# The eight blocks of each recurrence turn in 512-column matmuls, with VectorE adding the halves

## The chip, the cores and the metric

The kernel runs on one core of a Trainium2 chip. The core has TensorE (PE in the profile; its weight loads are PEld), VectorE (DVE), ScalarE (ACT), GpSimd (POOL) and SyncE (SP), which issues most transfers. The metric is the device time of one launch in microseconds. Three runs of the kernel before took 3868.46 to 3870.62 us, median 3868.93.

## What is computed

Two blocks of a network on 256 tokens of width 2048, in float32. The part that matters here is the first block, which has two layers; each projects the normed input to the inputs of a gated delta rule with 16 heads of width 128, and runs it in chunks of 64 tokens:

```python
h = rmsnorm(x, norm_w) * (1.0 + scale[:, None, :]) + shift[:, None, :]
u = h @ w_in
qkv_a, beta_a, a_a, z_a, q_b, k_b, v_b, z_b, g_a, g_b = split_cols(u, SPLIT_SIZES)
qkv_a = jax.nn.silu(causal_conv(qkv_a, conv_w)).astype(jnp.float32)
...
q_a = l2norm(q_a) * (GDN_HEAD_DIM ** -0.5)
k_a = l2norm(k_a)
...
o_a = gated_delta_rule(q_a, k_a, v_a, g, beta)
o_a = rmsnorm(o_a, gdn_norm_w).reshape(b, s, GDN_WIDTH).astype(x.dtype) * jax.nn.silu(z_a)
```

Sliding-window attention, output products and a second block follow; the change doesn't touch them.

## The kernel before

**Products in parts.** A float32 product of weights W and activations x is made of fp32r parts: W is split into `Wh` and `Wl` = W - `Wh`, and x into a high and a low part. Three products count: `Wh`·x_high, `Wh`·x_low and `Wl`·x_high. The activations lie in `H` as [slab, part, token], so that the high and low parts of a slab of 128 rows are 512 adjacent columns. There are two forms. `pe_half` (L262) makes three 256-column matmuls per slab (L283, L284, L285) and sums all three in the left 256 columns of a PSUM bank. `pe_wide` (L288) makes one 512-column matmul (L300: `Wh` against both parts; the low part's product falls in the right half of the bank) and one of 256 columns (L301: `Wl` against the high part, into the left half). The bank's halves then have to be added, which `dve_tile` (L345, L349) does with a VectorE sum of 512 elements to 256.

**The stream.** Weights come in blocks of 128 output columns by 2048 rows, 8 KB per partition, and each block is worked in two halves of 8 slabs. SyncE fetches blocks into the four places of `raw`. ScalarE casts a half to `Wh` (`act_cast`, L356), VectorE subtracts (`dve_low`, L362), and TensorE multiplies. `Wh` and `Wl` are rings of four halves. While TensorE works on half n, ScalarE and VectorE prepare half n + 4 into the place that TensorE left last. A finished block stands in bank `G[b % 2]`; whoever takes it out increments `tile_taken`, and TensorE begins the block after next only then.

**A turn of the recurrence.** `pe_gdn`, `act_gdn`, `dve_gdn` and `pool_gdn` run side by side. For each of the two layers there are nine turns: the first (`chain` false) only makes projections, the next seven (a loop, `fresh` and `chain` true) make the projections of head pair i while the delta rule of pair i - 1 runs between them, and the ninth (`fresh` false) makes eight gate blocks beside the last pair's delta rule. A turn has eight blocks (q, k and v for two heads each go to `cin`, z to `zin`), so 16 halves, n = 0 to 15. The chain's steps are written into the halves by hand: `before(n)`, `between(n)` after four slabs, `after(n)` after six. In halves 2 to 6 the inverse of a 64 x 64 triangular block is doubled in size: TensorE L1077 makes a product, VectorE masks it (L1330), TensorE L1106 makes a second, VectorE puts it in place with a predicated copy (L1361) and sums it (L1365) for the next half's L1077. Half 8 gives the state (`S`, L1383), half 9 and 10 `vn` (L1339) and the output (L1056), half 12 the squares' sums of the next pair's q and k (`sq_lo`, L1434, then L1135), half 14 the normed q and k (`qkn`, L1419), with which the next turn begins (the gram product, L1064). The conv steps of the next pair (L1312, L1315) fill VectorE's remaining places.

**Order.** Each engine works its instructions in written order. ScalarE takes out each of the eight blocks: in odd halves, after its cast, it copies the left 256 columns to `cin` or `zin` (L1251), or in the ninth turn takes tanh of them (L1256). In a chained turn VectorE's `dve_low` runs one half late: iteration n holds that of half n - 1, and the sixteenth stands behind the loop. At the end of a fresh turn ScalarE waits until the last block is taken (L1258).

## Time and profile before

| | |
|---|---|
| median of three runs | 3868.93 us |
| profiled execution | 3868.1 us |
| its span | 3866.3 us |
| TensorE busy | 3729.4 us, 96% |
| VectorE busy | 2856.1 us, 74% |
| ScalarE busy | 1905.5 us, 49% |
| a chained turn of the recurrence | 61.8 us |

Times in the rows below are in microseconds from the start of the span. A row of the timeline gives start, duration, engine, line of the kernel, operation, what is written and read, the shape, and how many equal ones it merges; in brackets stands the idle time of the engine before it and what ended it. TensorE's matmuls overlap in the trace (each lasts longer than the distance to the next), so its pace is read from start to start. A row of the busy table gives the stretch, its length, and busy time (with the number of instructions) of PE, PEld, DVE, ACT and POOL, then the granted clock, the share of the transfer engines and GB/s.

### The profile page before, as it was taken

To read this page: it belongs to the slowest core of one execution; us is meant where nothing else is said; L and a number is where in the kernel's file an instruction comes from. 1 tells how busy PE (TensorE), PEld (TensorE's weight loads), DVE (VectorE), ACT (ScalarE), POOL (GpSimd) and SP (SyncE) were. 2 spreads that over 40 slices of the span, in tenths; PEclk is the share of its full clock that TensorE was granted. 3 is DMA by queue.
4 is the path that set the end of the run, shared out by engine and by line. 5 is a ranking of instruction groups with operands and counts; after the bars stand their busy time and mean duration, and the time that the engine had idled before them with its cause. 6 is when DMAs were issued, how large, how long until landed. Compare 5 with 4: busy or idle time off the path is not lost.

```text
span 3866.3 us, 70292 instructions
## 1 busy us (share of the span) xinstructions
PE 3729.4 (96%) x27254; PEld 3491.6 (90%) x27254; DVE 2856.1 (74%) x3924; ACT 1905.5 (49%) x2898; POOL 175.7 (5%) x184
## 2 busy tenths in 40 slices
PE   1999999999999999999999999999999999999998
PEld 1999999899988999999989998999987899989988
DVE  8788887867779778888686776665576666666676
ACT  1556565335544355555534554454565433434365
POOL 0111111000000012121000000000000000000000
PEclk8999999999999999999999999999999999999999
DMA  9544444864468844434486444544534555555543
GB/s 396 177 149 146 142 146 139 303 234 164 157 234 318 299 148 142 150 137 152 146 317 214 158 157 175 186 169 175 183 124 149 185 185 185 185 185 185 185 146 127
DMA packets 138700, 720.49 MB, mean 186 GB/s; under 512 B 37697, under 2 KB 38145, under 8 KB 62337
## 3 DMA queue, kind: packets, MB, share of 16 engines
q1 hardware_dynamic: 111456, 631.31, 45.8%
q10 hardware_dynamic: 27040, 86.32, 6.6%
q8 instruction: 146, 2.39, 0.2%
q14 instruction: 58, 0.47, 0.0%
HBM read 711.22 MB, written 2.16 MB: 185 GB/s over the span
## 4 chain that ended last, share of the span: by engine, by line
PE 75%; DVE 13%; issue 5%; ACT 4%; DMA 2%; DVEq 1%; ACTq 0%; SPq 0%
PE bank L300 17%; PE bank L283 11%; PE bank L284 11%; PE bank L285 11%; PE bank L301 9%; DVE Wl L362 3%; PE bank L2416 2%; PE bank L2415 2%; PE bank L2414 2%; ACT Wh L356 2%; DMA raw<-in_ada 1%; DVE gm_more L1315 1%; PE bank L1077 1%; PE bank L326 1%; PE bank L322 1%
## 5 line engine op out<-in xcount | busy, mean ns | idle before, releaser
L356 ACT CAST Wh<-raw 128x1024 fp32r<-128x1024 f32 x1124 | 1170.9, 1047 | 1603.2 <-PE bank L285 905.6
L362 DVE TENSOR_TENSOR Wl<-raw,Wh 128x1024 fp32r<-128x1024 f32 x1124 | 1380.0, 1231 | 701.4 <-ACT Wh L356 698.9
L283 PE MATMUL bank<-H,Wh 128*128 128x256 f32 x4928 | 1444.9, 293 | 2.0 <-DVE Wl L362 1.2
L284 PE MATMUL bank<-H,Wh 128*128 128x256 f32 x4928 | 1393.8, 283 | 0.0
L285 PE MATMUL bank<-H,Wl 128*128 128x256 f32 x4928 | 1393.1, 283 | 0.0
L283 PEld LDWEIGHTS bank<-H,Wh 128*128 128x128 f32 x4928 | 942.4, 191 | 24.6 <-issue 13.7
L284 PEld LDWEIGHTS bank<-H,Wh 128*128 128x128 f32 x4928 | 943.0, 191 | 8.0 <-issue 4.8
L285 PEld LDWEIGHTS bank<-H,Wl 128*128 128x128 f32 x4928 | 942.1, 191 | 0.0
L300 PE MATMUL bank<-H,Wh 128*128 128x512 f32 x2112 | 746.9, 398 | 4.6 <-DVE WS L349 4.5
L301 PE MATMUL bank<-H,Wl 128*128 128x256 f32 x2112 | 592.6, 281 | 0.0
L300 PEld LDWEIGHTS bank<-H,Wh 128*128 128x128 f32 x2112 | 396.7, 188 | 103.2 <-DVE Wl L362 5.7
L301 PEld LDWEIGHTS bank<-H,Wl 128*128 128x128 f32 x2112 | 398.9, 189 | 0.0
L300 PE MATMUL bank<-O,Wh 128*128 128x512 f32 x896 | 317.2, 397 | 6.6 <-DVE both L349 6.3
L301 PE MATMUL bank<-O,Wl 128*128 128x256 f32 x896 | 251.0, 280 | 0.0
L300 PEld LDWEIGHTS bank<-O,Wh 128*128 128x128 f32 x896 | 168.0, 188 | 50.1 <-DVE Wl L362 6.8
L2415 PE MATMUL bank<-O,Wh 128*128 128x256 f32 x704 | 199.2, 283 | 0.0
L2416 PE MATMUL bank<-O,Wl 128*128 128x256 f32 x704 | 199.2, 283 | 0.0
L2414 PE MATMUL bank<-O,Wh 128*128 128x256 f32 x704 | 199.2, 283 | 0.0
L301 PEld LDWEIGHTS bank<-O,Wl 128*128 128x128 f32 x896 | 169.2, 189 | 0.0
L2414 PEld LDWEIGHTS bank<-O,Wh 128*128 128x128 f32 x704 | 135.1, 192 | 0.5
L2416 PEld LDWEIGHTS bank<-O,Wl 128*128 128x128 f32 x704 | 135.1, 192 | 0.0
L2415 PEld LDWEIGHTS bank<-O,Wh 128*128 128x128 f32 x704 | 135.1, 192 | 0.0
(413 smaller groups left out, 4169.8 us busy)
## 6 DMA issues: line engine op xcount, KB each, us to landing
raw<-in_stream SPq DMA_DIRECT2D x560, 1024.0 KB, 4.8
WS<-in_ada ACTq DMA_DIRECT2D x94, 512.0 KB, 6.3
raw<-in_ada SPq DMA_DIRECT2D x32, 1024.0 KB, 7.5
gm_more<-in_ada ACTq DMA_DIRECT2D x20, 512.0 KB, 7.4
WS<-rows_d ACTq DMA_DIRECT2D x16, 512.0 KB, 5.2
KR<-in_ada ACTq DMA_DIRECT2D x14, 512.0 KB, 7.2
raw<-in_stream SPq DMA_DIRECT2D x8, 512.0 KB, 6.9
gm_more<-WS ACTq DMA_DIRECT2D x32, 128.0 KB, 4.8
```

The lines of the kernel that those rows point to most:

```text
L283: pe.matmul(out[:, 0:T], wh, xh[:, kt, :], start=first, stop=False)
L284: pe.matmul(out[:, 0:T], wh, xl[:, kt, :], start=False, stop=False)
L285: mm = pe.matmul(out[:, 0:T], wl, xh[:, kt, :], start=False, stop=last)
L300: pe.matmul(out[:, :], wh, x[:, kt, :, :], start=kt == 0, stop=False)
L301: mm = pe.matmul(out[:, 0:T], wl, x[:, kt, 0, :], start=False, stop=kt == KT - 1)
L322: pe.matmul(out[:, :], wh, x[:, kt, :, :], start=first, stop=False)
L326: mm = pe.matmul(out[:, 0:T], wl, x[:, kt, 0, :], start=False, stop=last)
L356: act.copy(Wh[:, n % 4, :], raw[:, (sbk + 2) % 4, k * (D // 2):(k + 1) * (D // 2)]).then_inc(hi_ready, 1)
L362: dve.tensor_tensor(Wl[:, n % 4, :], raw[:, (sbk + 2) % 4, k * (D // 2):(k + 1) * (D // 2)], Wh[:, n % 4, :].bitcast(F32), ALU.subtract).t ...
L2414: pe.matmul(o, wh, ah, start=x == 0, stop=False)
L2415: pe.matmul(o, wh, al, start=False, stop=False)
L2416: m = pe.matmul(o, wl, ah, start=False, stop=x == 3)
```

## The change

The eight blocks of a fresh turn use `pe_wide` in place of `pe_half`; `pe_wide` learns to call `between` and `after` at the same slabs. ScalarE no longer copies these blocks out. VectorE does, with `dve_tile`, right behind the `dve_low` of the block's second half: in a chained turn that is in even iterations (block b in iteration 2b + 2) and, for block 7, behind the loop. The writes wait for the reads of the turn before (the conv's last step, and `zs` for block 6). The ninth turn keeps `pe_half` and ScalarE's tanh, which now waits on `tile_taken` for its first block, since VectorE took the block before.

```diff
--- before.py
+++ after.py
@@ -285,7 +285,7 @@
                 mm = pe.matmul(out[:, 0:T], wl, xh[:, kt, :], start=False, stop=last)
             mm.then_inc(half_used, 1)
 
-        def pe_wide(pe, q, sbk, k, fill, bank, x, tiles=None):
+        def pe_wide(pe, q, sbk, k, fill, bank, x, tiles=None, between=None, after=None):
 
             out = G[bank]
             pe.wait_ge(lo_ready, q * 8 + (2 * sbk + k + 1))
@@ -293,6 +293,10 @@
                 pe.wait_ge(tile_taken, fill + 1)
             s = (2 * sbk + k) % 4
             for j in range(KT // 2):
+                if j == KT // 4 and between:
+                    between()
+                if j == KT // 4 + 2 and after:
+                    after()
                 kt = k * (KT // 2) + j
                 if tiles and kt % 4 == 0:
                     tiles(kt // 4)
@@ -1154,7 +1158,10 @@
                 if chain:
                     before(n)
                 b, k = n // 2, n % 2
-                pe_half(pe, q + b // 4, b % 4, k, l * TILES + 4 + i * 8 + b, b % 2, Hh, Hl, between=lambda: between(n), after=lambda: after(n))
+                if fresh:
+                    pe_wide(pe, q + b // 4, b % 4, k, l * TILES + 4 + i * 8 + b, b % 2, H, between=lambda: between(n), after=lambda: after(n))
+                else:
+                    pe_half(pe, q + b // 4, b % 4, k, l * TILES + 4 + i * 8 + b, b % 2, Hh, Hl, between=lambda: between(n), after=lambda: after(n))
 
         def act_gdn(act, l, i, fresh, chain):
             S, F, q = st_gdn, st_fr, l * Q_LAYER + Q_PRE + 2 * i
@@ -1243,15 +1250,10 @@
                     front(n)
                 b, k = n // 2, n % 2
                 act_cast(act, q + b // 4, b % 4, k)
-                if k and fresh:
-                    if chain and b == 6:
-                        S.wait(act, "dve", "zs", r)
-                    act_tile(act, q + b // 4, b % 4)
-                    dst = cin[:, b, 3:3 + T] if b < 6 else zin[:, b - 6, :]
-                    act.copy(dst, G[b % 2][:, 0:T]).then_inc(tile_taken, 1)
-                elif k:
+                if k and not fresh:
                     if b == 0:
                         F.wait(act, "dve", "qkn", r)
+                        act.wait_ge(tile_taken, l * TILES + 4 + i * 8 + 2)
                     act_tile(act, q + b // 4, b % 4)
                     act.activation(gates8[:, b, :], G[b % 2][:, 0:T], ACT.Tanh, scale=0.5).then_inc(tile_taken, 1)
             if fresh:
@@ -1421,6 +1423,15 @@
                     F.wait(dve, "act", "tanh_v", f)
                     F.done(dve.scalar_tensor_tensor(cs[:, 4:6, :], tv, 1.0, cs[:, 4:6, :], ALU.add, ALU.mult), "dve", "silu_v")
 
+            def tile(b):
+
+                if chain and b < 6:
+                    F.wait(dve, "dve", f"conv{b}_3", r)
+                if chain and b == 6:
+                    S.wait(dve, "dve", "zs", r)
+                dst = cin[:, b, 3:3 + T] if b < 6 else zin[:, b - 6, :]
+                dve_tile(dve, q + b // 4, b % 4, l * TILES + 4 + i * 8 + b, b % 2, dst)
+
             for n in range(16):
                 if chain:
                     before(n)
@@ -1432,15 +1443,19 @@
                             continue
                         F.wait(dve, "act", f"sq{h}", f)
                         F.done(dve.tensor_tensor(sq_lo[h], tm2[:, 2 * h:2 * h + 2, :], sq_hi[h].bitcast(F32), ALU.subtract), "dve", f"sq_lo{h}")
-                if n or not chain:
-                    late = 1 if chain else 0
+                late = 1 if chain else 0
+                if n >= late:
                     dve_low(dve, q + (n - late) // 8, (n - late) // 2 % 4, (n - late) % 2)
+                if fresh and n >= late and (n - late) % 2:
+                    tile((n - late) // 2)
                 if chain:
                     after(n)
                 if fresh:
                     front(n)
             if chain:
                 dve_low(dve, q + 1, 3, 1)
+                if fresh:
+                    tile(7)
```

In the program of the kernel before, VectorE's rows around the subtraction in half 2 of the looped turn (Wl from raw and Wh), then the predicated copy of the doubling step:

```order
L361 REGISTER_ALU
L362 TENSOR_TENSOR Wl<-raw,Wh 128x1024 [waits hi_ready]
L121 REGISTER_ALU
L1360 MEMSET SEC_X 1x1 [waits gdn_pe_done]
L1361 COPY_PREDICATED WS<-C,bank 128x128x2
L121 REGISTER_ALU
L1365 TENSOR_REDUCE WS<-WS 128x32x2 [waits gdn_dve_done]
```

The same place in the kernel after:

```order
L365 REGISTER_ALU
L366 TENSOR_TENSOR Wl<-raw,Wh 128x1024 [waits hi_ready]
L351 REGISTER_ALU [waits gdn_front_dve_done]
L352 ISA [waits half_used]
L353 TENSOR_REDUCE Y<-bank 128x256 [waits tile_taken]
L121 REGISTER_ALU
L1362 MEMSET SEC_X 1x1 [waits gdn_pe_done]
L1363 COPY_PREDICATED WS<-C,bank 128x128x2
L121 REGISTER_ALU
L1367 TENSOR_REDUCE WS<-WS 128x32x2 [waits gdn_dve_done]
```

The sum of the bank's halves (L353) now stands between the subtraction and the predicated copy.

VectorE at half 14 of the looped turn, before, with the subtraction for half 13, `qkn` (Y from gm_more) and the next subtraction:

```order
L361 REGISTER_ALU
L362 TENSOR_TENSOR Wl<-raw,Wh 128x1024 [waits hi_ready]
L121 REGISTER_ALU
L121 REGISTER_ALU [waits gdn_front_act_done]
L1419 TENSOR_TENSOR Y<-gm_more 128x1024 [waits gdn_pe_done]
L361 REGISTER_ALU
L362 TENSOR_TENSOR Wl<-raw,Wh 128x1024 [waits hi_ready]
```

And after:

```order
L365 REGISTER_ALU
L366 TENSOR_TENSOR Wl<-raw,Wh 128x1024 [waits hi_ready]
L121 REGISTER_ALU
L353 TENSOR_REDUCE Y<-bank 128x256 [waits tile_taken,half_used,gdn_dve_done]
L121 REGISTER_ALU
L121 REGISTER_ALU [waits gdn_front_act_done]
L1421 TENSOR_TENSOR Y<-gm_more 128x1024 [waits gdn_pe_done]
L365 REGISTER_ALU
L366 TENSOR_TENSOR Wl<-raw,Wh 128x1024 [waits hi_ready]
```

The sum of block 6 stands ahead of `qkn`, L1421 in the new numbering.

ScalarE at the end of the looped turn, before, with the casts of halves 14 and 15, the copy of block 7, the loop's branch and the first steps of a turn:

```order
L355 REGISTER_ALU [waits raw1_landed]
L356 CAST Wh<-raw 128x1024 [waits half_used]
L1251 COPY Y<-bank 128x256 [waits half_used]
L1258 ISA
L2714 REGISTER_ALU [waits tile_taken]
L2714 COMPARE_AND_BRANCH
L1171 ACTIVATE WS<-Y 128x512
L1172 ACTIVATE WS<-WS 128x512
```

And after:

```order
L359 REGISTER_ALU [waits raw1_landed]
L360 CAST Wh<-raw 128x1024 [waits half_used]
L1260 ISA
L2729 REGISTER_ALU [waits tile_taken]
L2729 COMPARE_AND_BRANCH
L1178 ACTIVATE WS<-Y 128x512
L1179 ACTIVATE WS<-WS 128x512
```

The copy is gone; the wait on `tile_taken` before the branch stays and is now for VectorE's sum of block 7.

## Rows read from the trace of the kernel before

**Rows 1.** The page: busy time of each engine in the whole span.

```profile
PE 3729.4 (96%) x27254; PEld 3491.6 (90%) x27254; DVE 2856.1 (74%) x3924; ACT 1905.5 (49%) x2898; POOL 175.7 (5%) x184
```

**Rows 2.** Busy table of the chained turn from 313.86 to 375.65 us.

```profile
313.86:375.65 61.79, 61.73 (x494) 59.83 (x492) 53.71 (x83) 35.90 (x58) 10.12 (x11) 1.00 0.41 145
```

**Rows 3.** Timeline, TensorE, narrow form; columns start us, duration us, engine, line, operation.

```profile
148.16 0.28 PE L283 MATMUL bank<-H,Wh 128*128 128x256 f32 x1
...
149.60 0.28 PE L283 MATMUL bank<-H,Wh 128*128 128x256 f32 x1
```

**Rows 4.** Timeline, TensorE, wide form in an end stage.

```profile
714.28 0.39 PE L300 MATMUL bank<-O,Wh 128*128 128x512 f32 x1
...
715.67 0.39 PE L300 MATMUL bank<-O,Wh 128*128 128x512 f32 x1
...
799.66 0.40 PE L300 MATMUL bank<-H,Wh 128*128 128x512 f32 x1
...
802.84 0.40 PE L300 MATMUL bank<-H,Wh 128*128 128x512 f32 x1
```

**Rows 5.** Lines L349 and L1251: duration ns min/median/max.

```profile
L349 DVE TENSOR_REDUCE WS<-bank x120: 679/683/692, 740.9 to 3693.1; 128x256 f32<-128x512 f32 x120
...
L1251 ACT COPY Y<-bank x128: 357/366/381, 148.6 to 1867.7; 128x256 f32<-128x256 f32 x128
```

**Rows 6.** Timeline, VectorE, halves 2 and 4 of that turn.

```profile
323.35 1.21 DVE L362 TENSOR_TENSOR Wl<-raw,Wh 128x1024 fp32r<-128x1024 f32 x1
325.00 0.73 DVE L1361 COPY_PREDICATED WS<-C,bank 128x256 f32<-128x256 int32 x1 [0.44 <-issue]
...
331.65 1.23 DVE L362 TENSOR_TENSOR Wl<-raw,Wh 128x1024 fp32r<-128x1024 f32 x1 [0.16 <-ACT Wh L356]
333.04 0.43 DVE L1361 COPY_PREDICATED WS<-C,bank 128x256 f32<-128x256 int32 x1 [0.17 <-issue]
...
333.51 0.64 DVE L1365 TENSOR_REDUCE WS<-WS 128x64 f32<-128x256 f32 x1
```

**Rows 7.** Timeline, TensorE, first product of halves 3 and 5.

```profile
326.44 0.70 PE L1077 MATMUL bank<-WS 128*128 128x256 f32 x2
...
334.26 0.64 PE L1077 MATMUL bank<-WS 128*128 128x256 f32 x2
```

**Rows 8.** Timeline, VectorE, halves 8 to 12.

```profile
349.02 1.21 DVE L362 TENSOR_TENSOR Wl<-raw,Wh 128x1024 fp32r<-128x1024 f32 x1
350.85 0.42 DVE L1383 COPY Y<-bank 128x256 f32<-128x256 f32 x1 [0.62 <-PE bank L1048]
...
356.39 0.41 DVE L1339 TENSOR_TENSOR WS<-WS,bank 128x256 f32<-128x256 f32 x1
...
359.05 1.28 DVE L1312 TENSOR_SCALAR Y<-Y,PAR 128x256 f32<-128x256 f32 x1
...
363.90 1.28 DVE L1434 TENSOR_TENSOR O<-gm_more,O 128x512 fp32r<-128x512 f32 x2
```

**Rows 9.** Timeline, TensorE: output product, squares' sum, next turn's gram.

```profile
356.86 0.49 PE L1056 MATMUL bank<-Y 128*128 128x128 f32 x2
...
365.24 0.50 PE L1135 MATMUL bank<-O,ones_r 128*128 128x512 f32 x1
...
375.65 0.60 PE L1064 MATMUL bank<-Y 128*128 128x128 f32 x3
```

**Rows 10.** Timeline, ScalarE's cast and VectorE's last steps, half 13.

```profile
372.17 1.03 ACT L356 CAST Wh<-raw 128x1024 fp32r<-128x1024 f32 x1
...
373.23 1.22 DVE L362 TENSOR_TENSOR Wl<-raw,Wh 128x1024 fp32r<-128x1024 f32 x1 [1.53 <-ACT Wh L356]
374.38 1.22 DVE L1419 TENSOR_TENSOR Y<-gm_more 128x1024 f32<-128x1024 f32 x1
```

**Rows 11.** Timeline, ScalarE, the four n_of copies at half 1.

```profile
320.21 1.26 ACT L1177 COPY WS<-WS 32x128 f32<-32x128 f32 x4
```

**Rows 12.** Timeline, TensorE, squares' sum of an unchained first turn.

```profile
175.43 1.98 PE L1138 MATMUL bank<-gm_more,C 128*128 128x512 f32 x4 [0.47 <-ACT gm_more L1222]
```

## The prediction, written before the result was known

> **What bounds the kernel now.** I read the page's engine times first: TensorE is busy for 96% of the span, VectorE for 74%, ScalarE for 49% [rows 1]. That average says nothing about the stage that is edited, so the second view is the busy table of one turn of the recurrence, from one gram product (L1064) to the next. A turn takes 61.79 us; in it TensorE is busy for 61.73, VectorE for 53.71 and ScalarE for 35.90, at a granted clock of 1.00 [rows 2]. So TensorE sets the time of a turn and hardly waits, and VectorE has 8.1 us left. The third view, the timelines of the two engines side by side, says how much of this is usable: TensorE's chain products start only some hundredths of a microsecond after the VectorE instruction they need has ended. In half 5 the product starts at 334.26 and its operand was done at 333.51 + 0.64 = 334.15 [rows 6, 7]. VectorE's free time lies in front of those instructions, not behind them. That balance is what the change touches from both sides: it takes work from TensorE and gives work to VectorE.
>
> **Part 1: 512-column matmuls.** Per slab of 128 rows three 256-column matmuls become one of 512 and one of 256. The columns stay at 768, and at 2.4 GHz they are 0.320 us. The gain is in what a matmul costs beyond its columns. Narrow: four slabs take 149.60 - 148.16 = 1.44 us, 0.360 each [rows 3]. Wide, in a stage that has this form already: four slabs take 1.39 us (0.3475 each) in one place and nine take 3.18 us (0.3533 each) in another [rows 4]. I take the middle, 0.350. A turn has 16 halves of 8 slabs, so 128 x 0.010 = 1.28 us per turn, 0.08 us per half, with bounds of 0.86 and 1.60 from the two wide rows. Sixteen turns have the change (eight in each layer; the ninth, which brings the gates, keeps the narrow form): 16 x 1.28 = 20.5 us if nothing else moved.
> The Trainium skill (TensorE: Matmul & The Clock Gate, "Back-to-back issue gap") gives N/2.4 + 2.5 ns for a matmul of N columns. By it a slab would go from 327.5 to 325.1 ns, and all sixteen turns would gain 5 us, not 20. The page's gap is too short here for the narrow form (109 ns against 120) and for the wide; this trace decides, and the sum keeps its own rows.
>
> **Part 2: VectorE adds the halves.** Eight adds of 512 elements a turn. The same instruction runs in other stages in 0.679 to 0.692 us, 0.683 in the middle [rows 5]. Back to back a following instruction starts about 0.07 before the printed end of the one ahead (373.23 + 1.22 against 374.38) [rows 10], so a tile costs VectorE 0.61, eight of them 4.9 us a turn. VectorE would be at 53.7 + 4.9 = 58.6 of some 61: it fits by sum, and the question is place. I walk through a chained turn (14 of the 16), tile by tile; "shift" is how much later than before an event comes, counted from the turn's gram. TensorE alone would come 0.08 earlier with each half.
> - Tile 0 stands in half 2 between the Wl subtraction at 323.35 and the predicated copy at 325.00, which waited 0.44 for TensorE [rows 6]. The subtraction comes 0.25 earlier, so the tile is over by 323.10 + 1.15 + 0.61 = 324.86. Hidden. The copy itself moves up with its product, the next product at 326.44 [rows 7] has shift -0.14.
> - Tile 1, half 4: the subtraction starts as its cast is done, 0.22 earlier than 331.65; 331.43 + 1.15 + 0.61 = 333.19, where the copy was at 333.04 [rows 6]. The copy is 0.15 later, and so is the product at 334.26: shift +0.1, where TensorE alone would be at -0.3. The first 0.4 is lost.
> - Tile 2, half 6, has the same place in a half whose other VectorE work is shorter (no sum behind the copy). I count it as hidden; no row of mine shows that room.
> - Tile 3, half 8: 349.02 + 1.15 + 0.61 = 350.78, and VectorE sat idle for 0.62 before 350.85 [rows 8]. Hidden. But from there to half 12 VectorE has no wait left. The subtraction for `vn` can't start before 356.39 - 0.06, so TensorE's output product at 356.86 [rows 9] has shift -0.06 and the gain of five halves is lost again.
> - Tile 4, half 10, lands in that full stretch: the squares' low part, done at 363.90 + 1.28 = 365.18, comes 0.55 later, and TensorE waits for it with its squares' sum at 365.24 [rows 8, 9]. One thing can take some of it back: the conv step at 359.05 lasts 1.28 us for 256 elements, for which a predicated copy takes 0.43 [rows 6, 8]. Something holds it up there (GpSimd, I take it), and it may shrink as it moves. Shift +0.45, bounds +0.3 and +0.55.
> - Tile 5, half 12, is behind that. VectorE later waits 1.53 us for the cast of half 13 [rows 10], and the tile is hidden in it.
> - Tile 6, half 14: that cast ends at 372.17 + 1.03 and is followed by the subtraction and `qkn`, with the next turn's gram right behind (374.38 + 1.22 = 375.60, gram at 375.65) [rows 9, 10]. The tile now stands between them: +0.61 with no cover. The cast itself depends on the squares' sum (+0.45) but ScalarE has shed a copy of 0.27 ahead of it and had some slack, so I give it +0.04.
> - Tile 7 ends some 0.7 us after the last subtraction. ScalarE must now wait for it at the end of the turn, since its closing wait is on `tile_taken`, and queued behind that wait are the tanh of z, the exp, the cast of half 0 and the four `n_of` copies. Those ended at 320.21 + 1.26 = 321.47 [rows 11], and by my reckoning will end at 321.7, as TensorE arrives for them. No cost yet, and no slack left.
> Sum of a chained turn: 0.04 + 0.61 = 0.65 us longer. The lower bound is +0.34 (ScalarE gives back its 0.27), the upper +1.2 (the +0.55 of tile 4 goes through to the cast as well). 14 x 0.65 = 9.1 us, bounds 4.8 and 17.
>
> **Part 3: ScalarE's copies.** 128 copies of 0.366 us go [rows 5]. ScalarE is busy for 36 of 62 us in a turn, so this is worth the 0.27 named above (a copy back to back) and nothing more.
> GpSimd and SyncE lose and gain no instruction. Of their common access to memory the Trainium skill (GPSIMD Engine Reference, "Specifications") says that it collides with VectorE instructions of two SBUF inputs or a two-port mode. The tile reads one PSUM bank, so by that rule its 0.68 would stand beside GpSimd too. No row here shows this line beside GpSimd, and the sum doesn't need it.
>
> **Part 4: the two unchained first turns.** There the tiles precede conv, tanh, SiLU and the squares' sum, for which TensorE waited 0.47 already [rows 12]. Four tiles of 0.61 before it would cost up to 1.3 us net of the gain; free VectorE time would leave the gain of 1.28. I take +0.5 each, +1 in all, bounds -2.6 and +2.6.
>
> **The sum.** 9.1 + 1.0 = 10.1 us more. The profiled execution took 3868.1 us (span 3866.3), which gives 3878.2; the median of the three runs is 0.8 above it, so 3879. By the bounds: 4.8 - 2.6 = +2 and 17 + 2.6 = +20, thus 3871 to 3889.
>
> **Rivals.**
> *The full gain.* VectorE had 8.1 us free [rows 2] and gets 4.9 more. If the casts and low parts run further ahead than I think, as the ring of four half slabs allows, only the gain is left: 3868.9 - 20.5 = 3848; with half the stalls about 3858. Against it stand the starts at 334.26, 365.24 and 375.65, each within 0.11 us of VectorE's end. It decides at tile 6: only if `qkn` is not the last thing that gram waits for. Chance 0.15.
> *Balance.* Lost and gained are equal within 7 us: tile 4 is absorbed by the shrinking conv step, ScalarE is earlier by its copies, the unchained turns keep their gain. 3862 to 3876; chance 0.20.
> *ScalarE late at the start of the turn.* The point at which it decides is tile 7: if it is done more than 0.1 us later than I count, each tenth delays `n_of` and the first product of half 2, and the casts behind. With the tile's own 0.6 us going through, 14 x 1.25 + 1 = 18.5, 3887; chance 0.25.
> My forecast keeps 0.40, of which about 0.13 falls under +7.7 us.
>
> **The numbers.** A measurement of this kernel tells 0.2%, 7.7 us, from no change. Faster than that: 0.15 (the first rival). Within: 0.20 + 0.13 = 0.33. Slower: 0.27 + 0.25 = 0.52. The likeliest case alone spans 3871 to 3889. For 8 in 10 the range takes in most of the balance case, the better part of the third rival, and the near half of the first: 3857 to 3896.
>
> **What the profile will show.** Right: 2048 slabs in the wide form in the turns, 128 more VectorE adds of about 0.68 us; a turn of 62.4 us instead of 61.8; TensorE waits of 0.3 to 0.6 us in front of the product of half 5, the output product, the squares' sum and the gram; VectorE busy 58 to 59 us a turn; ScalarE's tanh of z waiting for tile 7. Wrong: a turn of 60.5 us with no such waits (the full gain), a turn above 63 with a wait in front of half 2 (third rival), or a tile much longer than 0.68 us. A pitch of the wide form beside the chain's own products outside 0.346 to 0.354 would make part 1 wrong.

## The result

The changed kernel takes 3897.02 us (median of four runs, 3896.28 to 3899.08), the kernel before 3869.77 in the same comparison: a ratio of 1.0072 with a 95% interval of 1.006 to 1.0084, or 27 us more. The forecast was slower, 3879; the time lies 1 us above the range (3857 to 3896).

The page's engine times and the busy table of one chained turn, from gram to gram (columns as in [rows 2]):

```profile
PE 3732.5 (96%) x25206; PEld 3383.6 (87%) x25206; DVE 2934.6 (75%) x4052; ACT 1873.2 (48%) x2770; POOL 176.8 (5%) x184
```

```profile
319.40:383.07 63.67, 61.70 (x363) 52.71 (x364) 58.09 (x91) 33.95 (x50) 10.10 (x11) 1.00 0.38 139
```

A turn is 63.67 us, against 61.79 [rows 2]. TensorE's busy time hardly moved (the profile counts the overlap of its matmuls as busy); it is idle for 2 us. VectorE went from 53.71 to 58.09 busy, ScalarE from 35.90 to 33.95. All fourteen chained turns are alike: 63.15 to 63.68 us from gram to gram, 63.56 in the mean. Fourteen times 1.76 is 25 us, and the two first turns have 4 us more, as told below. Together that is 29 us; the medians are 27 us apart, the two profiled executions 31.

TensorE's waits in that turn, from its timeline (idle time and what ended it in brackets; the numbers of the lines are those of the changed kernel, L1081 is the product of the doubling step, L1115 that of half 7, L1060 the output, L1139 the squares' sum, L1068 the gram):

```profile
319.40 0.38 PE L1068 MATMUL bank<-Y 128*128 128x128 f32 x1 [0.36 <-DVE Y L1421]
...
327.76 0.49 PE L1081 MATMUL bank<-WS 128*128 128x256 f32 x1 [0.31 <-ACT WS L1184]
...
340.43 0.48 PE L1081 MATMUL bank<-WS 128*128 128x256 f32 x1 [0.18 <-DVE WS L1367]
...
351.24 0.43 PE L1115 MATMUL bank<-WS 128*128 128x64 f32 x2 [0.23 <-DVE WS L1324]
...
363.46 0.38 PE L1060 MATMUL bank<-Y 128*128 128x128 f32 x1
...
372.33 0.51 PE L1139 MATMUL bank<-O,ones_r 128*128 128x512 f32 x1 [0.59 <-DVE O L1445]
...
383.07 0.38 PE L1068 MATMUL bank<-Y 128*128 128x128 f32 x1 [0.51 <-DVE Y L1421]
```

In the kernel before, the list of TensorE's waits over these turns is empty. Put side by side from each turn's gram, averaged over eight chained turns (the third to the sixth of each layer), the landmarks come later than before by:

| | predicted | changed kernel |
|---|---|---|
| product of half 2 | -0.16 | +0.27 |
| product of half 3 | -0.14 | +0.36 |
| product of half 5 | +0.1 | +0.60 |
| product in half 7 | (not given) | +0.99 |
| output product, half 10 | -0.06 | +1.03 |
| squares' sum, half 12 | +0.45 | +1.50 |
| next gram | +0.65 | +1.83 |

A matmul's record lasts longer than the distance to the next one (0.28 us against 0.12), so a wait of up to some 0.15 us doesn't show as idle time. From start to start it does. The next table has the time from the start of the last matmul of the weights to the start of the chain product behind it, in us, as means over the same eight turns:

| in front of | kernel before | wide form alone (below) | changed kernel |
|---|---|---|---|
| product of half 2 | 0.12 | 0.12 | 0.54 |
| product of half 5 | 0.12 | 0.12 | 0.44 |
| product in half 7 | 0.12 | 0.12 | 0.51 |
| output product, half 10 | 0.14 | 0.33 | 0.34 |
| squares' sum, half 12 | 0.18 | 0.33 | 0.86 |
| next gram | 0.14 | 0.39 | 0.70 |

The changed kernel waits 2.6 us a turn more than the kernel before. Its faster slabs take 1.0 of that back, and 0.3 more is lost right behind the products that waited.

VectorE's timeline at halves 2, 4 and 6, at half 7, from the state copy of half 8 to `vn`, and at halves 10 to 12 (L353 is the sum of a bank's two halves, L1363 the predicated copy, L1367 the sum behind it, L1324 the copy that half 7's product needs, L1385 the state copy, L1341 `vn`, L1410 SiLU, L1314 and L1317 conv steps, L1445 the low part of the squares):

```profile
329.99 0.68 DVE L353 TENSOR_REDUCE Y<-bank 128x256 f32<-128x512 f32 x1
330.92 0.73 DVE L1363 COPY_PREDICATED WS<-C,bank 128x256 f32<-128x256 int32 x1 [0.25 <-issue]
...
338.70 0.68 DVE L353 TENSOR_REDUCE Y<-bank 128x256 f32<-128x512 f32 x1
339.31 0.43 DVE L1363 COPY_PREDICATED WS<-C,bank 128x256 f32<-128x256 int32 x1
...
339.77 0.61 DVE L1367 TENSOR_REDUCE WS<-WS 128x64 f32<-128x256 f32 x1
...
346.77 0.69 DVE L353 TENSOR_REDUCE Y<-bank 128x256 f32<-128x512 f32 x1
347.38 0.44 DVE L1363 COPY_PREDICATED WS<-C,bank 128x256 f32<-128x256 int32 x1
...
348.06 1.47 DVE L1317 SCALAR_TENSOR_TENSOR gm_more<-Y,PAR,gm_more 128x256 f32<-128x256 f32 x1 [0.23 <-DVE WS L1363]
349.45 1.27 DVE L1314 TENSOR_SCALAR gm_more<-Y,PAR 128x256 f32<-128x256 f32 x1
350.75 0.43 DVE L1324 COPY WS<-bank 64x256 f32<-64x256 f32 x1
...
357.45 0.43 DVE L1385 COPY Y<-bank 128x256 f32<-128x256 f32 x1
...
363.00 0.41 DVE L1341 TENSOR_TENSOR WS<-WS,bank 128x256 f32<-128x256 f32 x1
...
364.46 0.69 DVE L353 TENSOR_REDUCE Y<-bank 128x256 f32<-128x512 f32 x1
365.06 1.90 DVE L1410 SCALAR_TENSOR_TENSOR gm_more<-gm_more 128x1024 f32<-128x1024 f32 x1
366.89 1.39 DVE L1314 TENSOR_SCALAR Y<-Y,PAR 128x256 f32<-128x256 f32 x1
368.42 0.49 DVE L1317 SCALAR_TENSOR_TENSOR Y<-Y,PAR 128x256 f32<-128x256 f32 x1
...
370.99 1.29 DVE L1445 TENSOR_TENSOR O<-gm_more,O 128x512 fp32r<-128x512 f32 x2
```

The sum takes 0.68 us as it did elsewhere [rows 5]. In half 2 it is covered: 0.25 us of the wait before the copy is left of 0.44 [rows 6]. In half 4 the copy follows it directly, and TensorE waits for the sum behind it (339.77 + 0.61, product at 340.43).

### The profile page after: what moved, and what is told of

It reads as the page before. It is cut to its first block, busy times and chain, and to the rows that moved or that the text cites. A ratio compares the mean times of both kernels' runs of the same rounds, so it can differ in the third digit from the quotient of the medians.

```text
span 3897.3 us, 66380 instructions
## 1 busy us (share of the span) xinstructions
PE 3732.5 (96%) x25206; PEld 3383.6 (87%) x25206; DVE 2934.6 (75%) x4052; ACT 1873.2 (48%) x2770; POOL 176.8 (5%) x184
## 4 chain that ended last, share of the span: by engine, by line
PE 71%; DVE 12%; issue 8%; ACT 6%; DMA 2%; DVEq 1%; ACTq 0%; SPq 0%
PE bank L304 20%; PE bank L305 10%; PE bank L283 8%; PE bank L284 8%; PE bank L285 8%; ACT Wh L360 3%; PE bank L2430 2%; PE bank L2431 2%; PE bank L2429 2%; DVE Wl L366 2%; DMA raw<-in_ada 1%; DVE gm_more L1317 1%; DVE Y L353 1%; PE bank L330 1%; PE bank L326 1%
## 5 line engine op out<-in xcount | busy, mean ns | idle before, releaser
L304 PE MATMUL bank<-H,Wh 128*128 128x512 f32 x4160 | 1513.5, 405 | 8.8 <-DVE WS L353 4.8
L304 PEld LDWEIGHTS bank<-H,Wh 128*128 128x128 f32 x4160 | 783.6, 188 | 196.9 <-DVE Wl L366 10.1
L283 PE MATMUL bank<-H,Wh 128*128 128x256 f32 x2880 | 831.2, 289 | 2.0 <-DVE Wl L366 1.2
L284 PE MATMUL bank<-H,Wh 128*128 128x256 f32 x2880 | 814.4, 283 | 0.0
L283 PEld LDWEIGHTS bank<-H,Wh 128*128 128x128 f32 x2880 | 551.6, 192 | 13.5 <-issue 9.3
L284 PEld LDWEIGHTS bank<-H,Wh 128*128 128x128 f32 x2880 | 551.9, 192 | 1.3 <-issue 0.5
L304 PE MATMUL bank<-O,Wh 128*128 128x512 f32 x896 | 316.7, 397 | 7.1 <-DVE both L353 7.0
L304 PEld LDWEIGHTS bank<-O,Wh 128*128 128x128 f32 x896 | 168.0, 188 | 50.7 <-DVE Wl L366 7.5
```

What stands on the lines that cost most here:

```text
L283: pe.matmul(out[:, 0:T], wh, xh[:, kt, :], start=first, stop=False)
L284: pe.matmul(out[:, 0:T], wh, xl[:, kt, :], start=False, stop=False)
L304: pe.matmul(out[:, :], wh, x[:, kt, :, :], start=kt == 0, stop=False)
```

## Experiments

Each kernel is compared with the kernel before on its own chip; the medians of the kernel before were 3867.4 to 3867.7. The changed kernel had a comparison of its own, in which the kernel before took 3869.77; where a run is said to take less or more than the changed kernel, two medians are subtracted, and the difference may be off by those 2 us. Landmarks are again from the gram, means over the same eight chained turns, "later" against the kernel before. Lists of waits are for the time from 250 to 670 us, which holds six to seven chained turns: total us, times, longest. `...` in a diff stands for lines left out.

### Each part alone

TensorE's part alone, on the kernel before, whose ScalarE and VectorE stay as they are:

```diff
...
+                if fresh:
+                    pe_wide(pe, q + b // 4, b % 4, k, l * TILES + 4 + i * 8 + b, b % 2, H, between=lambda: between(n), after=lambda: after(n))
...
```

> TensorE's part of the change alone: the fresh turns use the 512-column form, and ScalarE copies the left 256 columns out as in the kernel before; VectorE gets nothing. The product of Wh with the low part of the activations is left out of the eight blocks of a turn. Theory (the wide form is worth 1.03 us a turn, as the changed kernel's trace has it start to start: 44.93 us for the 128 slabs against 45.97): every chained turn 60.7 to 60.8 us, 16 turns 16 us, so about 3853. Rival (the wide form is no gain beside the chain's own products, or costs something at its seams): 3865 to 3875.

Measured: 3860.4 us, ratio 0.9982 (0.9973 to 0.9992): faster by 7 us, neither the 16 of the theory nor the rival. The turn is 61.33 us, 0.46 shorter. The landmarks come earlier all the way to the squares' sum (-0.17 at half 2, -0.26 at half 5, -0.42 at the output, -0.48 at the squares' sum), and then nothing more is gained (-0.46 at the gram). From all starts of this form in the changed kernel's trace, the 128 slabs take 44.93 us a turn against 45.97, so TensorE has 1.0 us less to do; not half of it gets through. The rest goes into waits for VectorE at three places, by the second table 0.19 us at the output product, 0.15 at the squares' sum and 0.25 at the gram. At the output product, the last matmul of the weights and the product behind it, first in the kernel before, then here:

```profile
356.72 0.28 PE L285 MATMUL bank<-H,Wl 128*128 128x256 f32 x1
356.86 0.38 PE L1056 MATMUL bank<-Y 128*128 128x128 f32 x1
```

```profile
354.65 0.28 PE L305 MATMUL bank<-H,Wl 128*128 128x256 f32 x1
354.98 0.49 PE L1060 MATMUL bank<-Y 128*128 128x128 f32 x2
```

At the gram, VectorE's timeline and the list of waits:

```profile
371.34 1.23 DVE L366 TENSOR_TENSOR Wl<-raw,Wh 128x1024 fp32r<-128x1024 f32 x1 [1.57 <-ACT Wh L360]
...
372.48 1.22 DVE L1426 TENSOR_TENSOR Y<-gm_more 128x1024 f32<-128x1024 f32 x1
```

```profile
PE bank L1068 <- DVE Y L1426: 0.7, 3, 0.2
```

The subtraction of half 13 waits for its cast (1.57 us idle), and TensorE waits for `qkn` behind it. So, with the order of instructions as it is, the turn has a second bound close below TensorE's: VectorE's queue from half 8 to half 12, then ScalarE's exponentials, the cast of half 13 and VectorE's `qkn`. The theory had the size of the part and not this bound.

VectorE's part alone, with 256-column matmuls (diff against the changed kernel; the values in `cin` and `zin` come out doubled):

```diff
...
-                dve_tile(dve, q + b // 4, b % 4, l * TILES + 4 + i * 8 + b, b % 2, dst)
+                dve.tensor_reduce(dst, G[b % 2][:, 0:T].unsqueeze(2).to_broadcast([P, T, 2]), AX.X, ALU.add).then_inc(tile_taken, 1)
...
```

> VectorE's part alone: 256-column matmuls as before, but VectorE takes the blocks out with a sum of 512 elements at the places of the changed kernel; it reads the left half of the bank twice, so the values in cin and zin are doubled. ScalarE has no copy. Theory (the cost is the place and length of VectorE's sums, whatever form TensorE uses): a chained turn of 62.9 to 63.6 us, 3888 to 3897. Rival (the cost needs the wide form, since only with its faster halves TensorE arrives early): turn 62.3, 3877 or less.

Measured: 3898.93 us, ratio 1.0079 (1.0063 to 1.0096), the turn 63.77, as the theory has it and a little beyond its range. The cost of the sums doesn't need the faster matmuls: it is all there without them (+1.98 us a turn), and with them it is +1.83. In this place the wide form gives 0.15 us of its 1.0.

### ScalarE at the start of the turn

The wait for the last sum and the tanh of z move from the start of the turn to half 2:

```diff
+            turn = l * TILES + 4 + i * 8 + 2
+
             def work(n):
                 if n == 0:
+                    S.done(act.activation(gb[:, 0], gb[:, 0], ACT.Exp), "act", "exp_gc")
+                if n == 2:
+                    act.wait_ge(tile_taken, turn)
                     S.done(act.activation(zs, zin, ACT.Tanh, scale=0.5), "act", "tanh_z")
-                    S.done(act.activation(gb[:, 0], gb[:, 0], ACT.Exp), "act", "exp_gc")
...
-            if fresh:
-                act.wait_ge(tile_taken, l * TILES + 4 + i * 8 + 8 + 2)
```

> The changed kernel, but ScalarE's wait for block 7 and the tanh of z stand in half 2 of the next turn, behind the n_of copies and two casts. Theory (the last sum holds ScalarE at the start of the turn, and with it n_of and the first product of half 2, 0.28 us later than before instead of 0.16 earlier): 0.3 to 0.44 us a turn, 3891 to 3893. Rival (the same lateness is waited for at a later VectorE step anyway): 3895 to 3898.

Measured: 3888.57 us, ratio 1.0055 (1.0038 to 1.0072), 8 us less than the changed kernel, a turn of 63.04, which is 0.58 less and more than the 0.3 to 0.44 expected. The product of half 2 comes at -0.17, exactly TensorE's own pace, and what is won stays won up to the squares' sum (+0.93 against +1.50). ScalarE's timeline in the changed kernel shows the step:

```profile
323.27 0.68 DVE L353 TENSOR_REDUCE Y<-bank 128x256 f32<-128x512 f32 x1
...
324.38 0.63 ACT L1178 ACTIVATE WS<-Y 128x512 f32<-128x512 f32 x1 [3.67 <-DVE Y L353]
...
325.44 1.03 ACT L360 CAST Wh<-raw 128x1024 fp32r<-128x1024 f32 x1
326.38 1.25 ACT L1184 COPY WS<-WS 32x128 f32<-32x128 f32 x4
```

The last sum ends at 323.95 and the tanh starts at 324.38, 0.43 later. Other steps of this turn, on TensorE, start 0.05 to 0.13 us after the one they wait for (340.43 after 340.38 at half 5); here the program has the end of the loop and its branch between wait and tanh, and the 0.43 is put down to them from this place in the order, as no run took them away. Then the cast of half 0 and the `n_of` copies follow without a gap to 327.63, and TensorE's product is at 327.76.

### Where the sums stand

Every sum behind the chain step that it stood ahead of (ScalarE as in the changed kernel):

```diff
-                if fresh and n >= late and (n - late) % 2:
-                    tile((n - late) // 2)
+                if fresh and not chain and n % 2:
+                    tile(n // 2)
                 if chain:
                     after(n)
+                if fresh and chain and n in (8, 10, 12):
+                    tile(n // 2 - 1)
                 if fresh:
                     front(n)
+                if fresh and chain and n in (2, 4, 7, 14):
+                    tile((n - 1) // 2 if n != 7 else 2)
```

> The changed kernel with each sum moved behind the chain step that it stood ahead of: in the chained turns, blocks 0, 1 behind the doubling step of halves 2 and 4, block 2 in half 7, block 3 behind the state copy, block 6 behind the normed q and k; blocks 4, 5 and 7 stay about where they were. Theory (the sums cost because of what is queued behind them): the waits in front of half 3 to 5's product, of the half 7 product and of the gram go, 1.4 us a turn, so 62.2 us a turn and 3877. Rival (VectorE has 4.9 us more to do and is simply full; places don't matter): not more than 5 us less than the changed kernel, 3891 to 3899.

Measured: 3906.41 us, ratio 1.0099 (1.0082 to 1.0116): 9 us worse than the changed kernel, where 20 less was expected. TensorE's waits:

```profile
PE bank L1081 <- ACT WS L1184: 5.8, 7, 0.9
PE bank L1060 <- DVE WS L1341: 3.9, 6, 0.7
PE bank L304 <- DVE Y L353: 3.4, 6, 0.7
PE bank L1139 <- DVE O L1445: 3.4, 6, 0.6
```

Read with the landmarks this is no case against the theory of places. The waits at half 5, half 7 and the gram are gone as expected (from half 2 to half 7's product the shift goes from +0.78 down to +0.71, where in the changed kernel it grows by 0.72). But three moved sums met another waiter: with block 6 behind `qkn` the last sum and ScalarE's tanh come later still (half 2 at +0.78); block 2's bank is needed at the start of half 8, and behind half 7's conv steps it is late (L304 waits for L353, 0.7 at most); block 3 behind the state copy delays `vn` for the output (L1060).

The same idea with these three repaired: the late tanh (its lines as above), block 2 ahead of half 7's conv steps, block 3 ahead of the state copy again. The diff is against the changed kernel.

```diff
...
-                if fresh and n >= late and (n - late) % 2:
-                    tile((n - late) // 2)
+                if fresh and (n % 2 if not chain else n in (8, 10, 12)):
+                    tile(n // 2 - (1 if chain else 0))
                 if chain:
                     after(n)
+                if fresh and chain and n in (2, 4, 7):
+                    tile(n // 2 - 1)
                 if fresh:
                     front(n)
+                if fresh and chain and n == 14:
+                    tile(6)
```

> The changed kernel with the late tanh of z and with the sums of blocks 0 and 1 behind the doubling step of halves 2 and 4, block 2 ahead of the conv steps of half 7, block 6 behind the normed q and k; block 3 stays ahead of the state copy, 4, 5, 7 stay too. Theory (only the place matters, each tile has one waiting instruction behind it, and the two that can't be moved here are those of halves 8 and 10): no waits at halves 3 to 5 and at half 7; a turn of 61.9 to 62.3, 3870 to 3878. Rival (VectorE is full, and work moved from one place is paid at the next): not below 62.8, 3885 to 3890.

Measured: 3870.3 us, ratio 1.0008 (0.9998 to 1.0017), 27 us less than the changed kernel (25 with each against its own kernel before), with the same instructions in another order. The turn is 61.69, 0.2 below what the theory expected, and one wait is left in the list:

```profile
PE bank L1139 <- DVE O L1447: 3.4, 6, 0.6
```

The landmarks are those of the wide form alone (-0.21, -0.25, -0.35 at half 2, 5 and the output) up to half 10; then comes the 0.57 us at the squares' sum. VectorE was not full: 4.9 us of sums find room in a turn that is no longer than before, though 0.36 longer than with the wide form alone.

### A shorter step

In the changed kernel, ScalarE copies the left half, VectorE adds the right half to it:

```diff
...
+                    act.copy(dst, G[b % 2][:, 0:T]).then_inc(left_in, 1)
...
-                dve_tile(dve, q + b // 4, b % 4, l * TILES + 4 + i * 8 + b, b % 2, dst)
+                dve.wait_ge(left_in, l * 64 + i * 8 + b + 1)
+                dve.tensor_tensor(dst, dst, G[b % 2][:, T:2 * T], ALU.add).then_inc(tile_taken, 1)
```

> The changed kernel with a shorter step at the same places: ScalarE copies the left half to cin or zin as before, and VectorE adds the right half of the bank to it, 256 elements (0.41 us, 0.34 start to start) in place of the sum of 512 (0.61). Nothing is left out. Theory (each microsecond that VectorE gets ahead of a chain step is paid in full where VectorE has no wait left): the cost at VectorE falls from 4.9 to 2.7 us a turn; of the 2.8 us of new waits less than half is left, so a turn of 62.1 to 62.4 and 3870 to 3877. Rival (the hand-over of the place, with its semaphores, costs and not the length): 63 to 63.6 a turn, 3890 or more.

Measured: 3882.57 us, ratio 1.0039 (1.0023 to 1.0054), a turn of 62.81. The direction is right, but the time is 5 us above the expected range: the waits at halves 5 and 7 are gone, but ScalarE has its copy of block 7 before the tanh as well, and half 2 is at +0.53.

> Both together: ScalarE's copy and VectorE's 256-element addition, at the better places, with the late tanh. Nothing is left out. Theory: what is left is 0.34 us at half 10 and the chain through q and k that held the run with the wide form alone to 61.33 us a turn; so 61.4 to 61.8, 3860 to 3868, no better than before or a few us better. Rival (the additions still fill VectorE and are paid in full, 2.7 us against 1.0 gained): 62.5 and more.

This one has both, the shorter step and the better places with the late tanh; its edits are those shown. Measured: 3866.47 us, ratio 0.9998 (0.9989 to 1.0007), a turn of 61.66, as expected. With the places right the shorter step is worth only 0.03 us a turn: between the output and the squares' sum it still loses 0.48. Most of the 3.8 us between the two medians lies in the first turns, which are 1.4 us shorter each.

### The first turns

The unchained first turns as in the kernel before, with the 256-column form and ScalarE's copy; the rest as in the changed kernel:

```diff
-                if fresh:
+                if fresh and chain:
                     pe_wide(...)
...
```

> The changed kernel, but the first, unchained turn of each layer keeps the 256-column form and ScalarE's copy. Theory (four sums stand ahead of conv, tanh, SiLU and squares, for which TensorE waited already, 1.9 and 2.8 us more up to the squares' sum in the changed kernel's trace): 4 us less than the changed kernel, 3893. Rival (the delay there is waited for later anyway): no difference.

Measured: 3892.65 us, ratio 1.0067 (1.0053 to 1.008), 4.4 below the changed kernel, as expected (2.2 with each against its own kernel before; the traces below have 4.1). From the product of `pe_keys` in half 1 to the squares' sum a first turn takes 30.1 and 30.3 us, as in the kernel before (30.3 and 30.2); in the changed kernel it is 32.1 and 33.0, less 0.2 to 0.35 that TensorE gains behind it. Most of it is lost at the start of half 8, and not at the squares' sum. In the changed kernel, layer 0 first, then layer 1:

```profile
165.77 0.68 DVE L353 TENSOR_REDUCE Y<-bank 128x256 f32<-128x512 f32 x1
...
166.59 0.47 PE L304 MATMUL bank<-H,Wh 128*128 128x512 f32 x1 [1.31 <-DVE Y L353]
...
178.03 0.70 PE L1142 MATMUL bank<-gm_more,C 128*128 128x512 f32 x1 [1.12 <-ACT gm_more L1229]
```

```profile
1425.89 0.68 DVE L353 TENSOR_REDUCE Y<-bank 128x256 f32<-128x512 f32 x1
...
1426.71 0.47 PE L304 MATMUL bank<-H,Wh 128*128 128x512 f32 x1 [2.58 <-DVE Y L353]
```

Block 4 can't begin until block 2 is out of its bank. ScalarE did that right behind its cast; VectorE comes to it only behind conv steps and two subtractions that take 3.87 us in layer 0 (161.97), where GpSimd is at work, and 2.35 later in the turn (169.35). In layer 1 TensorE's pace is lower after this wait. Busy table of the stretch behind it, then of the same place in layer 0:

```profile
1426.71:1429.50 2.79, 2.79 (x9) 2.40 (x10) 2.68 (x5) 0.00 (x0) 0.38 (x1) 0.57 0.78 247
...
166.59:169.40 2.81, 2.81 (x16) 2.44 (x17) 2.70 (x5) 0.00 (x0) 1.44 (x2) 1.00 0.74 277
```

After 2.58 us idle the granted clock was 0.57 in this stretch, which is mostly the lower of the two levels (1.2 GHz in place of 2.4), and slabs stood 0.64 us apart (starts at 1427.82 and 1428.46) in place of 0.35. Half 8 took 1.65 us longer by it (4.42 against 2.77 for the next half). After the 1.31 us of layer 0 it stayed at 1.00.

> The better places and the late tanh, and the first turn of each layer as before (narrow, copied by ScalarE). Theory: the first turns give back 2.8 us each against the run with the better places (32.9 up to the squares' sum against 30.2), the chained turns stay at 61.7: 3864 to 3866. Rival: the first turns' delay is absorbed, no change, 3870.

The same edit on top of the better places: 3866.0 us, ratio 0.9997 (0.9987 to 1.0007), 4.3 less than without, as expected.

### The last wait

On top of the run before (better places, narrow first turns), the conv steps of blocks 4 and 5 later and the sum of block 4 in half 11:

```diff
...
-                10: ((4, (0, 1)),), 11: ((4, (2, 3)),), 12: ((5, (0, 1)),), 13: ((5, (2, 3)),)}
+                11: ((4, (0, 1)),), 12: ((4, (2, 3)),), 13: ((5, (0, 1, 2, 3)),)}
...
```

> As the run before it in this call, and the last wait of TensorE in a chained turn is taken on: the sum of block 4 stands in half 11, the conv steps of block 4 in halves 11 and 12 and those of block 5 in half 13, so that two conv steps fewer stand ahead of the squares' low part. Theory (TensorE's 0.57 us at the squares' sum is VectorE's queue ahead of the low part, and the time behind it is free while VectorE waits for the cast of half 13): squares' sum 0.5 earlier, turn 61.1 to 61.3, 3856 to 3859. Rival (what moves behind the squares' sum delays the normed q and k by as much, as they are what held the wide form alone to 61.33): 61.6 to 62.0, 3864 to 3868.

Measured: 3870.53 us, ratio 1.0003 (0.9993 to 1.0013), a turn of 62.01: the rival, and 2.5 us beyond its range. The idle time at the squares' sum is gone from the list and stands at the gram:

```profile
PE bank L1068 <- DVE Y L1428: 2.1, 7, 0.4
PE bank L304 <- DVE Y L353: 0.5, 3, 0.2
```

> As the run with the later conv steps, but in the chained turns ScalarE copies the left half and VectorE adds the right half, 256 elements. Theory (VectorE is the full engine from half 8 to 14, and has 2.2 us less a turn): 60.8 to 61.2 us a turn, 3851 to 3856. Rival (the chain through ScalarE's exp, ln and casts to q and k sets the turn, and the copies lengthen it by 0.27 each): 61.3 to 61.7, 3858 to 3865.

With the 256-element addition in the chained turns: 3862.9 us, ratio 0.9988 (0.9978 to 0.9997), a turn of 61.43. That is the rival's range; the 60.8 to 61.2 of the theory would have needed more than the wide form alone gives. Here what moved behind the squares' sum fits in front of the cast of half 13, and the turn comes within 0.1 us of the wide form alone (61.33). It is the one run that leaves nothing out (its first turns keep the old form) and is faster than the kernel before, by 4.7 us with an interval that ends just short of no difference.

> The kernel before with only the later conv steps. Theory (in the kernel before TensorE's own work sets the turn, and no wait stands at the squares' sum): no gain, 61.8 us a turn or up to 0.4 more, 3867 to 3873. Rival (the later conv steps alone are the improvement): 3862 or less.

The later conv steps alone, in the kernel before: 3867.88 us, ratio 0.9999 (0.999 to 1.0009), a turn of 61.84, as expected. They are no gain by themselves; in the run above they make room for the additions.

## Why the prediction was right in sign and too small

**The bound.** That a turn is balanced, with VectorE's steps some hundredths ahead of TensorE's, was right, and so was the kind of cost: each sum delays the one step that TensorE waits for next, and the waits named (half 5, output, squares' sum, gram) are in the trace, with 0.32, 0.20, 0.68 and 0.56 us by the second table. The balance is closer than I read. The wide form alone ends at 61.33 us a turn, so with this order of instructions a full gain of 1.28 us was never there.

**Part 1.** The term was 1.28 us a turn of TensorE's time, and it measured 1.0. Slabs with no chain product between them stand 0.350 us apart in the wide form, as I took it from [rows 4], and 0.359 in the narrow form, where I had 0.360 (means of the eight turns); that makes 1.15, and the slabs next to a chain product gain less.

From half 5 to the output I let the shift fall by 0.16, with TensorE 0.44 us ahead of its old pace there and `vn` holding it. The wide form alone bears that out in kind: it gains 0.16 in that stretch (from -0.26 to -0.42), and its output product waits 0.19 longer for `vn` than before.

By the formula of the Trainium skill (TensorE: Matmul & The Clock Gate, "Back-to-back issue gap") the form gains 0.3 us a turn. That is further from the measured 1.0 than the rows were. The same section calls the formula the gap of an isolated matmul, which at small N leaves out the weight loads. Here each matmul has one (25206 of each on the page of the profile).

**Tile 7 and ScalarE, the step that failed most.** I had the `n_of` copies end at 321.7, which is 7.84 us from the gram, and so no cost; they end 8.23 from it (327.63 less 319.40). ScalarE starts its tanh 0.43 us after the last sum ends, and this 0.43 was to be read in the trace of before, in front of the same tanh. ScalarE's timeline there:

```profile
315.93 0.36 ACT L1251 COPY Y<-bank 128x256 f32<-128x256 f32 x1
316.72 0.63 ACT L1171 ACTIVATE WS<-Y 128x512 f32<-128x512 f32 x1 [0.43 <-ACT Y L1251]
```

The copy of block 7 ends at 316.29. Prediction: -0.16 at half 2; measured +0.27. The run with the late tanh gives it back to -0.17. It was my third rival; its cost is 0.43 to 0.58 us a turn, 6 to 8 us.

**Tile 2, called hidden.** It isn't. The two conv steps of half 6 stand behind it, beside GpSimd's work as before (they take 1.47 and 1.27 us, at 348.06 and 349.45, against 0.97 and 1.36), and the copy that half 7's product needs comes 1.5 us later from the gram than before. TensorE waits for it at 351.24, and the shift grows by 0.36 within half 7. I had said that no row showed that room. The runs with this sum in half 7 have no wait there.

**Tiles 1, 3, 4, 5, 6.** Half 2 to half 5: +0.26 predicted, +0.33 measured. Tile 3 is hidden. Output to squares' sum: +0.51 predicted, +0.47 measured. The conv step that I hoped would shrink didn't (1.28 before, 1.39 now). The one behind it did, from 1.35 to 0.49, but SiLU ahead of both grew from 1.23 to 1.90, as told in the last section. Squares' sum to gram: +0.20 predicted, +0.33 measured. Of the 0.41 that I let ScalarE give back here 0.28 came, about the copy's 0.27; the slack wasn't there, and its cast of half 12 waits 0.41 us for TensorE's late half.

**The first turns.** +1.0 us in all predicted (bound +2.6), +4.1 measured (1.6 and 2.5). I priced the four sums at the squares' sum alone and had no term for the bank: TensorE waits 1.31 and 2.58 us for block 2 to be taken out, and in layer 1 the lower clock behind that costs 1.65 more.

**The sum.** The turn was under-estimated by 1.18 us: 0.43 at its start (tile 7), 0.07 up to half 5, 0.59 from there to the output (0.36 of it tile 2; the rest wasn't regained, since from the state copy to `vn` VectorE takes 5.55 us in this kernel and 5.54 in the one before, and TensorE waits for it), -0.04 up to the squares' sum and 0.13 up to the gram. The upper bound of 1.2 us a turn was worked out from tile 4 alone and left these out. So the step that failed is the one that put tile 7 and tile 2 at no cost; they measured 0.43 and 0.36 us a turn, which is 11 of the 17 us by which the forecast of 10 us fell short.

## What to carry to other kernels

When an instruction is put into a full in-order engine, its cost is read at the step queued right behind it, and at the one that waits for its result; with the same instructions the kernel takes 27 us more than the kernel before or 3, by place alone. A wait at the end of a loop holds what the next pass does first, and the time over the branch has to be read from the trace. An engine that also frees a place, here a PSUM bank, can stop the busiest engine even where no result of it is waited for. And before a gain on the busiest engine is counted, ask for the second bound: here it lay 0.5 us below, and took half of the gain with nothing else changed. Waits shorter than the overlap of matmul records are found from start to start.

## What the runs showed of the hardware

The 512-column form gained 8 ns a slab beside the chain's products (1.0 us over 128 slabs) although it streams the same 768 columns.

SiLU (1024 elements, two SBUF inputs) takes 1.21 to 1.23 us in the chained turns of the kernel before and 1.90 in those of the changed kernel. What differs is who starts first, it or GpSimd. In the kernel before SiLU starts at 357.91, ahead of GpSimd, whose operation on a single element then lasts 1.08 us, until SiLU is over. With the sum ahead of SiLU (364.46), GpSimd starts first, its small operation lasts 0.18, and SiLU, from 365.06, is the one that is held up. First the kernel before, then the changed kernel:

```profile
358.10 1.08 POOL L1263 TENSOR_TENSOR SEC_X<-C 1x1 f32<-1x1 f32 x1 [10.25 <-PE bank L1057]
```

```profile
364.70 0.18 POOL L1265 TENSOR_TENSOR SEC_X<-C 1x1 f32<-1x1 f32 x1 [11.09 <-PE bank L1061]
364.85 1.03 POOL L1293 TENSOR_TENSOR WS<-TOK,WS 128x512 f32<-128x512 f32 x1
365.96 2.17 POOL L1295 TENSOR_TENSOR WS<-WS,C 128x512 f32<-128x512 f32 x1
```

In the runs that take the sum of block 4 away from there (the two with the later conv steps), SiLU is back at 1.22 us.

The sum itself, which reads PSUM, took 0.678 to 0.692 us in all 144 cases in `Y`:

```profile
L353 DVE TENSOR_REDUCE Y<-bank x144: 678/684/692, 152.3 to 2999.8; 128x256 f32<-128x512 f32 x144
```

The one at 346.77 has 0.6 of its 0.69 us beside this subtraction of GpSimd:

```profile
346.86 1.03 POOL L1293 TENSOR_TENSOR WS<-WS,TOK 128x512 f32<-128x512 f32 x1
```

Both agree with what the prediction cited of the Trainium skill (GPSIMD Engine Reference, "Specifications").
